# Expert stage: modulated rows are turned back and scattered, in place of modulation behind the gather

## What is computed

```python
h = _layer_norm(x) * (1.0 + sc2) + sh2
...
scores = jax.nn.sigmoid((t @ w_router).astype(jnp.float32))
...
hg = jnp.einsum('td,edf->tef', t, w_gate)
hu = jnp.einsum('td,edf->tef', t, w_up)
act = jax.nn.silu(hg) * hu * combine[..., None].astype(t.dtype)
y = jnp.einsum('tef,efd->td', act, w_down)
```

## Time and profile before

| | us |
|---|---|
| median of 3 runs | 3772.83 (3770.85 to 3775.89) |
| the profiled execution, its own time | 3756.39 |
| its span, first to last instruction | 3754.6 |
| PE busy | 3218.8 (86%) |
| DVE busy | 2410.4 (64%) |
| ACT busy | 1278.0 (34%) |
| POOL busy | 573.3 (15%) |

### The profile page before, as it was taken

One profiled execution on the slowest core, in us unless ns is written; L12 is line 12 of the kernel. 1 busy time (PEld: TensorE's weight loads), 2 busy tenths in 40 slices (PEclk: granted clock), 3 DMA queues, 4 the chain that ended last, 5 costly groups with the idle time before them and its releaser, 6 DMA issues. The chain is left out here.

```text
span 3754.6 us, 41065 instructions
## 1 busy us (share of the span) xinstructions
PE 3218.8 (86%) x14735; PEld 2557.3 (68%) x14735; DVE 2410.4 (64%) x3794; ACT 1278.0 (34%) x2024; POOL 573.3 (15%) x147
## 2 busy tenths in 40 slices
PE   4999977886699896788579789678999898989999
PEld 4767756664576685666467568566887687767887
DVE  6756575997676657699743746467765474564445
ACT  2323324764323333467321624232111322231111
POOL 0000001343000000243200000102443000004443
PEclk9999987998799998899779789888999899869999
DMA  7643535997654452799652034013442262102222
GB/s 257 220 166 109 198 98 186 338 334 261 207 177 163 150 171 85 249 335 338 232 199 86 23 99 133 27 62 107 135 155 91 101 189 94 64 23 90 91 99 79
DMA packets 289979, 583.95 MB, mean 156 GB/s; under 512 B 26233, under 2 KB 134209, under 8 KB 282748
## 3 DMA queue, kind: packets, MB, share of 16 engines
q1 hardware_dynamic: 277416, 537.87, 42.8%
q10 hardware_dynamic: 7764, 26.85, 1.8%
q0 software_dynamic: 4608, 16.78, 1.2%
HBM read 529.46 MB, written 78.71 MB: 162 GB/s over the span
## 5 line engine op out<-in xcount | busy, mean ns | idle before, releaser
L132 ACT CAST w_hi<-ring 128x2048 fp32r<-128x2048 f32 (+2 forms) x166 | 308.0, 1858 | 1210.2 <-PE ps L283 1031.1
L283 PE MATMUL ps<-hT_hi,w_hi 128*128 128x512 f32 (+1 forms) x1256 | 499.5, 398 | 26.4 <-DVEq L1117 12.5
L283 PE MATMUL ps<-hT_lo,w_hi 128*128 128x512 f32 (+1 forms) x1256 | 497.3, 396 | 0.0
L139 POOL TENSOR_TENSOR w_lo<-ring,w_hi 128x2048 fp32r<-128x2048 f32 x64 | 307.0, 4798 | 1022.2 <-ACTq L2778 636.8
L144 DVE TENSOR_TENSOR w_lo<-ring,w_hi 128x2048 fp32r<-128x2048 f32 (+3 forms) x112 | 245.4, 2195 | 240.5 <-ACT w_hi L132 240.2
L283 PE MATMUL ps<-hT_hi,w_lo 128*128 128x512 f32 (+1 forms) x1256 | 306.9, 396 | 7.1 <-DVE w_lo L144 7.1
L283 PEld LDWEIGHTS ps<-hT_hi,w_hi 128*128 128x128 f32 (+1 forms) x1256 | 238.1, 190 | 86.5 <-DVEq L1117 14.1
L283 PEld LDWEIGHTS ps<-hT_hi,w_lo 128*128 128x128 f32 (+1 forms) x1256 | 237.0, 189 | 64.6 <-DVE w_lo L144 8.8
L1054 DVE SCALAR_TENSOR_TENSOR piece_sums<-pieces,cond,piece_sums 128x512 f32<-128x512 f32 x294 | 220.8, 751 | 87.6 <-DMA pieces<-in_w_ada_dram 55.5
L283 PEld LDWEIGHTS ps<-hT_lo,w_hi 128*128 128x128 f32 (+1 forms) x1256 | 237.8, 189 | 55.3
L283 PE MATMUL ps<-w_hi,hT_hi 128*128 128x512 f32 (+1 forms) x672 | 259.9, 389 | 1.0 <-ACT w_hi L132 1.0
(11 more groups left out here) (590 smaller groups left out, 6568.1 us busy)
## 6 DMA issues: line engine op xcount, KB each, us to landing
ring<-in_mlp_w_dram SPq DMA_DIRECT2D x64, 1024.0 KB, 5.2
pieces<-in_w_ada_dram SPq DMA_DIRECT2D x96, 512.0 KB, 5.8
ring<-in_w_in_dram SPq DMA_DIRECT2D x36, 1024.0 KB, 7.1
pieces<-in_mod_w_dram SPq DMA_DIRECT2D x72, 512.0 KB, 5.0
raw_sep<-in_w_exp_gate_dram SPq DMA_DIRECT2D x50, 512.0 KB
raw_sep<-in_w_exp_up_dram SPq DMA_DIRECT2D x50, 512.0 KB
raw_sep<-in_w_exp_down_dram SPq DMA_DIRECT2D x24, 1024.0 KB
ring<-in_e_w_in_dram SPq DMA_DIRECT2D x24, 1024.0 KB, 5.5
```

Of the source, the lines that this page charges most:

```text
L132: self.k.nc.scalar.copy(self.k.parts[0][:, i, 0:words], self.k.ring[:, i, 0:words]).then_inc(self.high, 1)
L139: self.k.nc.gpsimd.tensor_tensor(self.k.parts[1][:, i, 0:words], self.k.ring[:, i, 0:words], self.k.parts[0][:, i, 0:words].bitcast(F32), ...
L283: mm = pe.matmul(out, a if weight_left else b, b if weight_left else a, start=first and part == 0 and q == ks[0] and o == 0, stop=last and ...
```

## The change

The modulation is no longer applied behind the gather. PE turns the modulated features `hT` back to rows, by products with an identity in fp32r (`rows_back`, four tiles; for each 128x128 piece one product with the high and one with the low part, added up in PSUM, 16 in all for a tile). ACT copies each tile from PSUM over the unmodulated one in `xn` (`row_tile`), and POOL scatters those rows, each tile after its copy (`x_rows_out`). Behind the gather, what PE's transposes leave in PSUM is the modulated feature block itself. So ACT makes the high part with one copy out of both banks (`features_high`), and DVE makes the low part with one subtraction that reads PSUM; `x_exact`, its eight activations and DVE's cast are gone, and with them `mod_pk` and its two loads. PE's features of a block now wait for DVE's subtraction of the block before (`xs_done`). The warm-up has 80 products for 100.

```diff
@@ router loads
-        sp.dma_start(cols.rearrange("(j p) -> p j", p=P), k.mod[:, 24:40], allow_slow_non_contiguous=True).then_inc(self.pk_landed, 16)
-        sp.wait_ge(self.pk_landed, 16)
-        sp.dma_start(self.pk[:], cols.rearrange("(i p k) -> p i k", i=2, k=KD)).then_inc(self.pk_landed, 16)
@@ moe, POOL
             for t in range(NT):
+                pool.wait_ge(x_rows_out, t + 1)
                 for i in range(2):
                     nc.gpsimd.indirect_dma_start(k.slots_x, bass.IndirectOffsetOnAxis(rows[:, i, t:t + 1], 0), xn[:, t, :], None).then_inc(scattered, 16)
@@ moe, PE
             mm.then_inc(score_t, 1)
+            def rows_back(t):
+                if t >= 2:
+                    pe.wait_ge(x_rows_out, t - 1)
+                for q in range(KD):
+                    o = back_banks(t)[:, q // 4, (q % 4) * P:(q % 4 + 1) * P]
+                    for a in range(2):
+                        mm = pe.matmul(o, hT[a][:, q, t * P:(t + 1) * P], ident_r[:], start=a == 0, stop=a == 1)
+                mm.then_inc(back, 1)
+
+            pe.wait_ge(ident_done, 1)
+            rows_back(0)
+            rows_back(1)
+            rows_back(2)
             pe.wait_ge(mask_done, 1)
...
             mm.then_inc(ranked, 1)
-            warm_up(k, pe, 7, 100)
+            rows_back(3)
+            warm_up(k, pe, 7, 80)
             def to_features(b):
                 pe.wait_ge(x_landed[b % 2], 16 * (b // 2) + 16)
                 if b >= 1:
-                    pe.wait_ge(ex_done, b)
+                    pe.wait_ge(xs_done, b)
@@ moe, ACT
-            def exact(b):
+            def features_high(b):
                 act.wait_ge(t_done, b + 1)
-                if b >= 1:
-                    act.wait_ge(xs_done, b)
-                for q in range(KD):
-                    last = nc.scalar.activation(ex[:, q, :], k.ps[:, 2 + q // 4, (q % 4) * P:(q % 4 + 1) * P], ACT.Identity,
-                                                scale=pk[:, 1, q:q + 1], bias=pk[:, 0, q:q + 1])
-                last.then_inc(ex_done, 1)
+                if b >= 2:
+                    act.wait_ge(unit_read, U.read("B", b - 2))
+                nc.scalar.copy(features(xT[b % 2][0]), k.ps[:, 2:4, :]).then_inc(xh_done, 1)
+
+            def row_tile(t):
+                act.wait_ge(back, t + 1)
+                nc.scalar.copy(xn[:, t, :].rearrange("p (b n) -> p b n", b=2), back_banks(t)).then_inc(x_rows_out, 1)
             nc.scalar.activation(sT[:], k.ps[0:N_EXP, 0, :], ACT.Sigmoid).then_inc(score, 1)
-            for s in range(EARLY):
+            row_tile(0)
+            split_high(0)
+            row_tile(1)
+            split_high(1)
+            row_tile(2)
+            row_tile(3)
+            for s in range(2, EARLY):
                 split_high(s)
@@ moe, DVE
+            V.tensor_copy(ident_r[:], k.ident[:]).then_inc(ident_done, 1)
             def split_x(b):
-                dve.wait_ge(ex_done, b + 1)
-                if b >= 2:
-                    dve.wait_ge(unit_read, U.read("B", b - 2))
+                dve.wait_ge(xh_done, b + 1)
                 hi, lo = xT[b % 2]
-                link(V.tensor_copy(hi[:], ex[:]))
-                V.tensor_tensor(lo[:], ex[:], hi[:].bitcast(F32), ALU.subtract).then_inc(xs_done, 1)
+                V.tensor_tensor(features(lo), k.ps[:, 2:4, :], features(hi).bitcast(F32), ALU.subtract).then_inc(xs_done, 1)
```

More of the change, by code:

```diff
@@ L1131, in __init__ @@
         self.steps, self.first_of, self.tri = sb("steps", [P, STEPS]), sb("first_of", [P, N_EXP, N_EXP]), sb("tri_sb", [P, P])
[L1132 removed]
     def signals(self, sems):
[L1135 removed]
+        self.landed, self.w_split = sems
     def load(self, sp):
         k = self.k
[L1139 removed]
         sp.dma_start(self.wr[:], k.A["w_router"].rearrange("(k p) e -> p k e", p=P)).then_inc(self.landed, 16)
@@ L1985, in moe @@
         sb = lambda n, s, t=F32: c.enter_context(nc.sbuf_tensor(fresh(n), s, t))
-        rb, before, first_of, tri, pk = router.rb, router.before, router.first_of, router.tri, router.pk
+        rb, before, first_of, tri = router.rb, router.before, router.first_of, router.tri
         more_rows, overflow, first_row, to_overflow = (router.steps[:, a:b] for a, b in ((0, 3), (3, 10), (10, 26), (26, 42)))
-        ones = sb("ones_r", [P, P])
+        ones, ident_r = sb("ones_r", [P, P]), sb("ident_r", [P, P], F32R)
         sc, sT = sb("sc_r", [P, NT, N_EXP]), sb("sT_r", [N_EXP, S])
@@ L2014, in part @@
             return hT[a][:, 4 * (q - 2):4 * (q - 1), :].rearrange("p k n -> p (k n)") if q < 4 else more[a][:, q - 4, :]
+        features = lambda ap: ap[:].rearrange("p (b q) n -> p b (q n)", b=2)
+        back_banks = lambda t: k.ps[:, 5:7, :] if t % 2 == 0 else k.ps[:, 0:2, :]
         gu = lambda a, s, kk: part(a, s).rearrange("p (g k n) -> p g k n", g=2, k=4)[:, :, kk, :]
-        (block, ones_done, score, score_t, mask_done, ranked, rows_done, of_done,
-         raw0, raw1, raw2, raw3, x0_landed, x1_landed, high, low_dve, low_pool, unit_read, t_done, ex_done, xs_done,
+        (block, ones_done, ident_done, score, score_t, mask_done, ranked, rows_done, of_done,
+         raw0, raw1, raw2, raw3, x0_landed, x1_landed, high, low_dve, low_pool, unit_read, t_done, xh_done, xs_done, back, x_rows_out,
          sg_done, act_done, at_done, ah_done, al_done, y_done, y0_stored, y1_stored, step) = c.enter_context(
-            stage(nc, "ones_done score score_t mask_done ranked rows_done of_done "
-                      "raw0 raw1 raw2 raw3 x0_landed x1_landed high low_dve low_pool unit_read t_done ex_done xs_done "
+            stage(nc, "ones_done ident_done score score_t mask_done ranked rows_done of_done "
+                      "raw0 raw1 raw2 raw3 x0_landed x1_landed high low_dve low_pool unit_read t_done xh_done xs_done back x_rows_out "
                       "sg_done act_done at_done ah_done al_done y_done y0_stored y1_stored step"))
@@ L2269, in _ @@
             link(V.tensor_tensor(nb[:], nb[:], start[:], ALU.add))
-            fit = ex[0:1].rearrange("p k n -> p (k n)")[:, 0:NO * N_EXP].rearrange("p (b e) -> p b e", e=N_EXP)
+            fit = eq[0:1].rearrange("p a b c -> p (a b c)")[:, 0:NO * N_EXP].rearrange("p (b e) -> p b e", e=N_EXP)
             link(V.tensor_tensor(fit, bcast(nb[0:1], 1, NO), bcast(overflow[0:1], 2, N_EXP), ALU.is_le))
```

12 lines of the change are left out of this document (4 added, 8 removed).

## The result

| | us |
|---|---|
| before, median of 3 | 3772.83 |
| changed, median of 3 | 3725.15 (3724.79 to 3732.15) |
| ratio, 95% interval | 0.9892 [0.9867, 0.9917] |
| profiled executions, before and changed | 3756.39, 3724.79 |

The kernel is faster by 47.7 us where 19.9 were forecast; the time lies 0.85 us under the range. So about 40 us is the better figure for the gain, with an interval of some 34 to 47.

The account below looks back on a forecast made before the run. The prediction took DVE and the DMA engines as nearly full, with DMA limiting the changed kernel. Its terms, -16.8 - 1.3 - 2.2 + 0.4 = -19.9 us, took 3772.8 to 3753 us, range 3726 to 3770.

Parts of the forecast that it names:

- Engines' round: Expert stage, steady blocks: engines alone would run at 11.33 us a block, 1.15 less than 12.48.
- DMA is late next: Expert stage, steady blocks: DMA engines, always busy, limit a block to 12.04 us; 8.4 us a layer gained.
- the row of 587 to 593 us: Profile window, first weights landing with PE, ACT, POOL almost idle: share 0.97 at 336 GB/s, read as DMA's limit.
- First and last block: Ends of the expert stage: first block gains 0.65 us a layer, last block 1.1 a layer.
- Ahead of the ranking: Turning three tiles back before the count: +0.2 us a layer, clock full near 591.7; upper bound +4.7 at low clock.
- Sum: Whole kernel, both layers: all terms together, -19.9 us, giving 3753 us.
- the steady part: Even blocks of the expert stage: 8.4 us a layer gained, 16.8 us in two layers.
- rival 1: Expert stage: DMA is no limit, 44 us gained instead of 16.8, kernel at 3726 us; chance 0.15.
- rival 2: Before the ranking: clock stays low, +4.7 us a layer instead of +0.2, kernel at 3762 us; chance 0.11.

Follow-up runs that it names:

- b_more_dma: The kernel before, reading each block's x rows a second time: pace 12.43 us a block, ratio 1.0003 to the kernel before.
- a_more_dma: The changed kernel, reading each block's x rows a second time: pace 11.55 us a block, ratio 0.9924 to the kernel before.
- the longer comparison: The changed kernel, unaltered, in five rounds against the kernel before: 3721.6 against 3761.6 us, ratio 0.9893.

## Why the prediction was wrong

- **Engines' round**, forecast 11.33 us a block with 12.48 before: 11.41. Right in size, and the durations were too: copy 1.02 (1.04 forecast), subtraction 1.21 (1.23). Its reason was half right. It took ACT's 1.6 to 1.87 and DVE's 0.69 as shared over two rounds of unequal length. In fact DVE's 0.69 counts in every round, and ACT's 1.89 gave only the 0.35 of waits behind half-clock stretches. That 1.15 lies so near the measured 1.07 is luck: ACT's part was taken too high and DVE's too low. The 5.10 of low C behind POOL was read, but the chain was not closed: low A, then POOL, then low C, with nothing of the three side by side.
- **"DMA is late next", 12.04 us a block: the step that failed**, 19.3 us gained a layer where it had 8.4. A share of 0.97 at 336 GB/s was taken for a ceiling, and the row of 587 to 593 us for a proof with idle engines. `b_more_dma` carried 379 GB/s and `a_more_dma` 406, and neither pace was set by it. The trace of the kernel before spoke against a ceiling already, in the two halves of that very row, whose shares differ by 0.04 and whose rates by 114 GB/s:

```profile
587.00:590.00 3.00, 0.42 (x4) 0.32 (x4) 2.08 (x6) 0.25 (x1) 0.00 (x0) 0.72 0.95 279
590.00:593.00 3.00, 0.00 (x0) 0.00 (x0) 2.62 (x12) 1.68 (x1) 0.00 (x0) 0.50 0.99 393
```

  The rule of the Trainium skill (HBM Reference, Specifications (TRN2)) of about 425 GB/s for a core alone was the better guide. The trace of `a_more_dma` comes to 406.
- **First and last block**, -0.65 and -1.1 a layer: first turn to first product took 6.02 instead of 6.96, -0.94, and the last part of the stage took 2.3 less in layer 0 and 1.8 in layer 1. Both had the right sign and were too small. Another 1.3 a layer came between the x rows and the even part, which the forecast did not have; its cause stays open.
- **Ahead of the ranking**, +0.2 a layer with the clock full near 591.7: +5.0 to +5.3, with the clock at half until 611.3. This is the second failed step; its upper bound, 4.7, was near. PE was busy from 588.6 on, as forecast, and the clock did not come back by it. The three tiles ended at 599.6, their products 0.21 us apart as at the low clock.
- **Sum**, both layers, from the two profiled executions: the steady part -38.6 (forecast -16.8), ahead of the ranking +10.3 (+0.4), the ends and what lies between -8.7 (-3.5), all else +5.4 (0). The two failed steps have opposite signs, so the total hides part of the error. What happened is rival 1 (DMA is no limit, -44 in the steady part) together with rival 2 (the clock stays low, +9.4). They had chances of 0.15 and 0.11, and their combination was not among the cases. That the median lands on rival 1's 3726 us is chance: the terms above come to -31.6, and the 40 us of the longer comparison would give some 3733.

## What to carry to other kernels

Don't take a DMA share near 1 for a ceiling. Here it was 0.97 at 336 GB/s, 1.00 at 379 and 1.02 at 406, in one and the same stage. Cut the row into shorter windows, or read the same bytes twice, before a bound is built on it. Where VectorE and GpSimd both subtract from SBUF, add their times up along the round and place what reads PSUM beside GpSimd's work. Price a product that is added to a waiting stretch at the clock that stands there. Look for waits that come back in some rounds only: eight waits of 0.72 to 0.88 us in the kernel before name the clock's share, which the means of a long window don't show. And when work ahead of a warm-up is moved, look whether the warm-up still ends in time.
